# Twenty identity products of TensorE between the two portions of a layer's last down matrices

## The chip, the cores and the metric

The kernel runs on one core of one Trainium2 chip. The metric is the device time of one execution in microseconds (us). The kernel before took 1609.62 us, the median of 3 runs (1609.38 to 1610.01).

## The reference: what is computed

Two layers of a hybrid decoder trunk work on 256 tokens of width 1024, all in 32-bit floats:

```
h = LayerNorm(alpha * x + Mixer(x))
x = LayerNorm(alpha * h + HierMoE(h))
```

The mixer projects x by one wide matrix, feeds retention and a selected sparse attention, gates and sums the two branches and projects the sum. HierMoE sends each token to one of 4 groups and to 2 of the 8 experts in it; each of the 32 experts is `(silu(x @ w_gate) * (x @ w_up)) @ w_down`, with matrices of 1024 by 512, 1024 by 512 and 512 by 1024.

## The kernel before, in words

The mixer part of a layer is bound by TensorE for most of its length; the weights stream through a ring of tiles and are split into a high and a low part by ScalarE and VectorE.

The expert part goes by quads, four experts at a time. Each expert has 32 slots for its tokens, so four experts fill the 128 columns of TensorE's array, and each matmul of a quad has its own 32 columns. Eight quads make a layer. For each quad the 24 MB of its matrices are loaded by SyncE's queue; `quad_half` multiplies the gate and the up matrices, ScalarE and VectorE make the hidden rows, TensorE transposes them (`bank_g`, then `hidT`), and `quad_half` with stage 2 multiplies the down matrices into `bank_y`, two banks of PSUM. `combine` then adds the weighted rows of the quad to the sum `acc`.

The last quad of a layer differs. `load_last_down` loads the second half of its four down matrices in two portions: first chunk 2 of all four experts (four transfers of 512 KB, counted by `last_in[0]`), then chunk 3 of all four (`last_in[1]`). `last_down` (line 1040 on) waits for one portion, multiplies it, waits for the other and multiplies that: for each chunk, 2 banks times 4 experts. Only after the second portion is multiplied does TensorE tell ScalarE that a bank of results is complete (`y_full`, line 1059); ScalarE copies it (line 1334), `sum_up_last` runs `combine` (line 1035) for each half of the columns, and VectorE's closing normalisation begins with statistics of the sum (line 1558). After layer 1 the normalised rows are transposed (line 873) and start layer 2; after layer 2 they are written out and the kernel ends.

TensorE's instructions run in the order in which they are written. `stay_warm(times, bank, of)` at line 615 exists already: it multiplies the identity (a 128 by 128 tile of the constant table) by itself into a bank that nobody reads. It is called with 19 and 3 at the start of layer 2, with 6 and 3 before the first quad, and with 8 on a cleared tile at the very start. The new call uses `bank_g`; its last reader, the copy of the transposed hidden rows, is over by then.

Of the kernel before, what the change touches and what calls it, by code (L numbers as in the profile page):

```python
# [27 lines left out]
FC = FF // P  # L28
# [133 lines left out]
def build(nc, x_in, w_in, w_ret_o, w_dsa_o, w_out, ln1_g, ln1_b, w_gate, w_up, w_down, ln2_g,  # L162
# [6 lines left out]
    with ctx:  # L169
# [133 lines left out]
        def banks(name):  # L303
# [4 lines left out]
        bank_g, bank_u = psum[:, 4, :], psum[:, 5, :]  # L308
# [33 lines left out]
                    for m, half in matrix_half]  # L342
        first_quad = [homes[v] if v in homes else ring_unit[v]
                      for _, v in sorted(FIRST_HOME.items())]
        first_in = [outside_in[v] if v in homes else unit_in[v]
                    for _, v in sorted(FIRST_HOME.items())]
        row_in = [sem(f"row_in{t}") for t in range(TT)]
        ident_in, table_in = sem("ident_in"), sem("table_in_mixer")
# [70 lines left out]
        def _(sp):  # L419
# [49 lines left out]
            for l in range(DEPTH):  # L469
                for name, i in STREAM.items():  # L470
# [3 lines left out]
                    if i < len(IN_TILES):  # L474
                        _, c, w = IN_TILES[i]
                        src = at(win_v, l)[:, :, c:c + w]
                    else:
                        v = {"dsa": dsa_v, "ret": ret_v, "out": out_v}[name[:3]]
                        n, w = int(name[3]), NB
                        k = KC * int(name[4]) if name[:3] == "ret" else 0  # L480
                        src = at(v, l)[:, k:k + KC, n * NB:(n + 1) * NB]
# [82 lines left out]
        def _(pe):  # L564
# [50 lines left out]
            def stay_warm(times, bank=bank_y[0], of=ident):  # L615

                for _ in range(times):
                    nc.tensor.matmul(bank[:, 0:P], of, of, start=True, stop=True)
# [426 lines left out]
            def last_down():  # L1045

                part = range(5 * QUAD, 6 * QUAD)
                for c in (FC - 2, FC - 1):
                    landed = last_in[c - FC // 2]
                    pe.wait_ge(landed, 16 * QUAD).then_inc(landed, -16 * QUAD)  # L1050
                    for n, bank in enumerate(bank_y):
                        for e, u in enumerate(part):
                            w = later_quad[u].rearrange("p (k n) -> p k n", k=FC // 2)
                            s = slice(e * SLOTS, (e + 1) * SLOTS)
                            mm = nc.tensor.matmul(bank[s, :], hidT[:, c, s],  # L1055
                                                  w[:, c - FC // 2, n * NB:(n + 1) * NB],
                                                  start=False, stop=(c == FC - 1))
                        if c == FC - 1:
                            mm.then_inc(y_full[n], 1)

            def experts(first=False, last=False, tiles=later_quad, landed=later_in):

# [43 lines left out]
                if last:  # L1106
                    last_down()
                else:
                    arrived(2, 1, landed)
                    quad_half(bank_y, hidT, FC, 2, 1, tiles)  # L1110
# [1001 lines left out]
```

## Time and profile before

| what | value |
|---|---|
| median of 3 runs | 1609.62 us (1609.38 to 1610.01) |
| the profiled execution, its own time | 1608.99 us |
| its span, first to last instruction | 1607.2 us |
| mean granted TensorE clock | 0.901 |
| TensorE matmuls busy | 1301.8 us, 81% |
| VectorE busy | 622.6 us, 39% |
| ScalarE busy | 387.9 us, 24% |
| DMA | 524.58 MB, mean 326 GB/s |

A busy share is an average over the whole span, and the stages of this kernel have different limits. In the 40 slices of the page, PE is the busy share of TensorE in tenths, PEclk the granted clock in tenths of full speed (1.00 is 2.4 GHz, 0.50 is 1.2 GHz), and DMA the share of the 16 DMA engines. A 32-bit product appears in the trace as two matmul records, each with its weight load, and is told in records below. A timeline row with "x38" stands for 38 records and its length reaches from the start of the first to the end of the last.

### The profile page before, as it was taken

What the parts mean: (1) busy time and instruction counts of PE and PEld (TensorE: products, weight loads), DVE (VectorE), ACT (ScalarE), POOL (GpSimd) and SP (SyncE); (2) the same over time, 40 slices, a digit from 0 to 9 for tenths busy, and PEclk for the clock granted to TensorE, in tenths of its full rate; (3) what the DMA queues carried; (4) which work ended last, traced back from release to release, by engine and by line L of the source; (5) the groups of instructions that cost most, each with busy time, mean ns of one, the idle gap of its engine ahead of it and who ended that gap; (6) DMA issues with size and microseconds to landing.
All of it is one profiled execution on the core that took longest, in us unless ns stands there. A gap on an engine that the chain in (4) does not pass through costs nothing. (4 is left out here: it accounts for less than half of the span.)

```text
span 1607.2 us, 21340 instructions
## 1 busy us (share of the span) xinstructions
PE 1301.8 (81%) x8678; PEld 883.9 (55%) x8678; DVE 622.6 (39%) x1063; ACT 387.9 (24%) x449; POOL 0.2 (0%) x4
## 2 busy tenths in 40 slices
PE   9999999999856656657799999999997556656665
PEld 8998889995312212222398988899953122212211
DVE  6788686654100100100187876765631000000102
ACT  4334634322100000001143357343220000000000
POOL 0000000000000000000000000000000000000000
PEclk9999999999977878877899999999999778788778
DMA  8555445789999999999954454376999999999996
GB/s 303 171 195 184 159 158 215 262 338 420 426 429 427 427 427 428 429 427 429 404 193 164 158 210 177 115 260 217 385 427 428 427 424 428 426 428 429 427 426 254
DMA packets 95686, 524.58 MB, mean 326 GB/s; under 512 B 5360, under 2 KB 9840, under 8 KB 65920
## 3 DMA queue, kind: packets, MB, share of 16 engines
q1 hardware_dynamic: 94864, 523.10, 80.8%
q8 instruction: 50, 0.82, 0.2%
q10 hardware_dynamic: 752, 0.50, 0.1%
q14 instruction: 20, 0.16, 0.0%
HBM read 522.53 MB, written 1.05 MB: 326 GB/s over the span
## 5 line engine op out<-in xcount | busy, mean ns | idle before, releaser
L1022 PE MATMUL psum<-ring,aqT 128*32 128x512 f32 x1536 | 275.3, 698 | 111.7 <-PEq L1010 111.7
L1672 DVE TENSOR_TENSOR w_low<-ring,w_high 128x2048 fp32r<-128x2048 f32 (+2 forms) x108 | 239.8, 2260 | 71.9 <-DVEq L1671 70.6
L1236 ACT ACTIVATE w_high<-ring 128x2048 fp32r<-128x2048 f32 (+2 forms) x108 | 198.6, 1886 | 193.3 <-ACTq L1232 178.8
L1022 PE MATMUL psum<-spare,aqT 128*32 128x512 f32 x256 | 131.9, 704 | 98.9 <-PEq L1077 98.9
L1909 DVE TENSOR_TENSOR qk<-psum,qk 128x512 f32<-128x512 f32 x16 | 11.1, 692 | 482.2 <-DVEq L1908 482.2
L1022 PEld LDWEIGHTS psum<-ring,aqT 128*32 128x32 f32 x1536 | 71.7, 126 | 214.3 <-issue 214.3
L1022 PE MATMUL psum<-rv,tmp 128*32 128x512 f32 x240 | 123.5, 705 | 68.1 <-PEq L1104 68.1
L701 PE MATMUL psum<-x_high,w_high 128*128 128x256 f32 x512 | 146.9, 287 | 0.0
L701 PE MATMUL psum<-x_high,w_low 128*128 128x256 f32 x512 | 143.4, 280 | 0.0
L701 PE MATMUL psum<-x_low,w_high 128*128 128x256 f32 x512 | 143.3, 280 | 0.0
L608 PE MATMUL psum<-w_high,x_high 128*128 128x512 f32 (+2 forms) x352 | 138.7, 394 | 0.0
L608 PE MATMUL psum<-w_high,x_low 128*128 128x512 f32 (+2 forms) x352 | 136.3, 387 | 0.0
L608 PE MATMUL psum<-w_low,x_high 128*128 128x512 f32 (+2 forms) x352 | 135.7, 385 | 0.0
L1022 PEld LDWEIGHTS psum<-spare,aqT 128*32 128x32 f32 x256 | 29.5, 127 | 188.9 <-issue 188.9
L1022 PE MATMUL psum<-rg,tmp 128*32 128x512 f32 x240 | 123.7, 706 | 0.0
L1022 PE MATMUL psum<-x_xT,tmp 128*32 128x512 f32 x240 | 123.7, 706 | 0.0
L1022 PE MATMUL psum<-ring,tmp 128*32 128x512 f32 x208 | 116.4, 723 | 0.0
L1022 PEld LDWEIGHTS psum<-rv,tmp 128*32 128x32 f32 x240 | 27.8, 127 | 146.1 <-issue 146.1
L701 PEld LDWEIGHTS psum<-x_high,w_high 128*128 128x128 f32 x512 | 96.3, 188 | 2.8 <-issue 2.8
L701 PEld LDWEIGHTS psum<-x_high,w_low 128*128 128x128 f32 x512 | 96.9, 189 | 1.4 <-issue 1.4
L701 PEld LDWEIGHTS psum<-x_low,w_high 128*128 128x128 f32 x512 | 96.0, 188 | 0.0
L1922 DVE TENSOR_TENSOR qk<-qk,psum 128x512 f32<-128x512 f32 x16 | 17.2, 1076 | 188.3 <-DVEq L1920 188.3
(260 smaller groups left out, 2294.4 us busy)
## 6 DMA issues: line engine op xcount, KB each, us to landing
ring<-in_w_gate_dram SPq DMA_DIRECT2D x56, 2048.0 KB, 33.1
ring<-in_w_in_dram SPq DMA_DIRECT2D x34, 2048.0 KB, 7.9
ring<-in_w_up_dram SPq DMA_DIRECT2D x28, 2048.0 KB, 22.2
spare<-in_w_up_dram SPq DMA_DIRECT2D x14, 2048.0 KB, 14.3
rv<-in_w_down_dram SPq DMA_DIRECT2D x12, 2048.0 KB, 31.2
rg<-in_w_down_dram SPq DMA_DIRECT2D x12, 2048.0 KB, 35.6
x_xT<-in_w_down_dram SPq DMA_DIRECT2D x12, 2048.0 KB, 40.1
ring<-in_w_down_dram SPq DMA_DIRECT2D x12, 2048.0 KB, 29.1
```

The source lines that it names most:

```text
L608: mm = nc.tensor.matmul(ps[:, t, 0:w], a, b[:, k, :], start=(k == 0 and m == 0), stop=(k == KC - 1 and m == 2))
L701: mm = nc.tensor.matmul(out, a[:, k, c], v, start=(start and k == 0 and m == 0), stop=(stop and k == KC - 1 and m == 2))
L1022: mm = nc.tensor.matmul(bank[s, :], lhs[:, c, s], w[:, k, n * NB:(n + 1) * NB], start=(c == 0), stop=(c == chunks - 1))
L1236: nc.scalar.activation(half_tile(high, i % HIGH, w, b), half_tile(ring, i % RAW, w, b), ACT.Copy).then_inc(high_ready, 1)
L1672: V.tensor_tensor(half_tile(low, i % RAW, w, b), half_tile(ring, i % RAW, w, b), half_tile(high, i % HIGH, w, b).bitcast(f32), ALU.subtrac ...
L1909: loop_step(V.tensor_tensor(msig, bank_g, msig, ALU.mult))
L1922: V.tensor_tensor(hid.rearrange("p (j q) -> p j q", j=FC), msig.rearrange("p (q j) -> p j q", j=FC), bank_u.rearrange("p (q j) -> p j q", ...
```

## The change

In `last_down`, inside the loop over the two chunks, after the matmuls of the first portion and so ahead of the wait for the second, TensorE is given twenty products of the identity with itself. The call is made once in each layer. Nothing is removed.

```diff
@@ last_down @@
                                                   start=False, stop=(c == FC - 1))
                         if c == FC - 1:
                             mm.then_inc(y_full[n], 1)
+                    if c == FC - 2:
+                        stay_warm(20, bank_g)
```

The function that it calls:

```
            def stay_warm(times, bank=bank_y[0], of=ident):

                for _ in range(times):
                    nc.tensor.matmul(bank[:, 0:P], of, of, start=True, stop=True)
```

## Rows read from the trace of the kernel before

**Rows 1.** The page: span, busy time by engine, and the 40 slices.
```profile
span 1607.2 us, 21340 instructions
PE 1301.8 (81%) x8678; PEld 883.9 (55%) x8678; DVE 622.6 (39%) x1063; ACT 387.9 (24%) x449; POOL 0.2 (0%) x4
PEclk9999999999977878877899999999999778788778
DMA  8555445789999999999954454376999999999996
```

**Rows 2.** The chain that ended last: start us, length us, what.
```profile
1590.59 1.92 PE psum L1055 x16
...
1592.54 3.69 PE psum L1035 x8
...
1603.97 0.75 DVE x_xT L1589
```

**Rows 3.** Timeline of TensorE, end of layer 1: start us, length us, operation.
```profile
789.05 0.59 PE L1055 MATMUL psum<-rv,tmp 128*32 128x512 f32 x1
...
793.02 0.68 PE L1055 MATMUL psum<-rv,tmp 128*32 128x512 f32 x1 [3.35 <-PEq L1050]
...
793.49 1.06 PE L1055 MATMUL psum<-rv,tmp 128*32 128x512 f32 x1
...
794.34 1.06 PE L1055 MATMUL psum<-rv,tmp 128*32 128x512 f32 x1
...
796.28 3.94 PE L1035 MATMUL psum<-qk,aqT 128*128 128x512 f32 x8
800.06 4.40 PE L618 MATMUL psum<-tab 128*128 128x128 f32 x38
804.70 0.63 PE L873 MATMUL psum<-tab,x_xT 128*128 128x128 f32 x4 [0.23 <-PEq L568]
```

**Rows 4.** Timeline of TensorE, end of layer 2.
```profile
1586.92 0.59 PE L1055 MATMUL psum<-rv,tmp 128*32 128x512 f32 x1
...
1587.35 0.59 PE L1055 MATMUL psum<-rv,tmp 128*32 128x512 f32 x1
...
1590.59 0.59 PE L1055 MATMUL psum<-rv,tmp 128*32 128x512 f32 x1 [2.62 <-PEq L1050]
...
1592.54 3.67 PE L1035 MATMUL psum<-qk,aqT 128*128 128x512 f32 x8
```

**Rows 5.** Timeline of VectorE: last statistics of layers 1 and 2.
```profile
800.26 0.70 DVE L1558 BATCH_NORM_STATS2 stat<-psum 128x6 f32<-128x512 f32 x1 [0.16 <-PE psum L1035]
...
1596.25 0.70 DVE L1558 BATCH_NORM_STATS2 stat<-psum 128x6 f32<-128x512 f32 x1 [0.16 <-PE psum L1035]
```

**Rows 6.** Windows: stretch, length, busy us by engine, granted clock, DMA share, GB/s.
```profile
789.50:793.00 3.50, 0.17 (x4) 0.01 (x1) 0.00 (x0) 0.00 (x0) 0.00 (x0) 1.00 1.03 391
793.50:796.50 3.00, 3.00 (x17) 0.75 (x10) 0.00 (x0) 0.60 (x1) 0.00 (x0) 0.50 1.05 385
800.00:804.50 4.50, 4.46 (x39) 4.21 (x37) 4.31 (x23) 0.74 (x1) 0.00 (x0) 1.00 1.07 383
808.00:812.00 4.00, 4.00 (x22) 3.13 (x20) 3.54 (x4) 2.89 (x4) 0.00 (x0) 1.00 0.10 29
1587.90:1590.50 2.60, 0.07 (x4) 0.00 (x0) 0.00 (x0) 0.00 (x0) 0.00 (x0) 1.00 0.47 189
1590.60:1592.50 1.90, 1.90 (x16) 0.46 (x16) 0.00 (x0) 0.60 (x1) 0.00 (x0) 1.00 0.00 0
```

**Rows 7.** Every record of line 618: durations ns min/median/max, first and last start.
```profile
L618 PEld LDWEIGHTS psum<-tab x80: 187/192/193, 366.2 to 1166.7; 128*128 128x128 f32 x80
L618 PE MATMUL psum<-tab x80: 272/275/356, 366.3 to 1166.9; 128*128 128x128 f32 x80
L618 PE MATMUL psum<-tmp x16: 294/421/582, 1.5 to 4.9; 128*128 128x128 f32 x16
```

**Rows 8.** Timeline of layer 2's start: a table load, a weight split, normalised rows.
```profile
796.57 1.64 SPq L447 DMA_DIRECT2D tab<-in_tables_dram  x1
...
798.84 1.90 ACT L1216 ACTIVATE w_high<-ring 128x2048 fp32r<-128x2048 f32 x1
...
803.64 0.75 DVE L1589 SCALAR_TENSOR_TENSOR x_xT<-x_xT,rstd,stage 128x512 f32<-128x512 f32 x1
...
806.37 1.17 PE L628 MATMUL psum<-w_high,x_high 128*128 128x512 f32 x4
```

## The prediction

> **What bounds the kernel now.** I read the 40 slices first [rows 1]. In both layers there is a long stretch in which the DMA digits are 9 and the granted clock is 7 or 8 tenths: the expert part, paced by the loading of its weights. Between them lies a stretch with DMA digits of 4 to 7 and a clock of 9: the mixer, where TensorE sets the pace. The change lies at the end of each expert part, so the second view is the chain that ended last [rows 2]. It has nothing to hide behind in layer 2: the second portion's matmuls (1590.59), the combining matmuls (1592.54), VectorE's normalisation and the output follow one another. Whatever delays 1590.59 delays the end by as much.
>
> The third view is TensorE's timeline around the wait for the second portion, once in each layer. In layer 1 the last records of the first portion start at 789.05 and those of the second at 793.02, after 3.35 us idle [rows 3]. In layer 2 it is 1587.35 and 1590.59, after 2.62 us idle [rows 4]. The two gaps differ in what the clock does behind them. Layer 1: granted clock 1.00 up to 793.0 and 0.50 from 793.5 to 796.5, that is 1.2 GHz. Layer 2: 1.00 through the gap and through the second portion, 2.4 GHz [rows 6]. So there is a clock loss to win back in layer 1 and, in this execution, none in layer 2.
>
> **The change: what the products cost.** Twenty calls are added in each layer. Line 618 shows how many records a call makes: 22 calls in layer 2's start and 9 before the first quad of each of two layers are 40 calls and 80 records [rows 7], so a call is 2 records and twenty are 40. The 38 records from 800.06 last 4.40 us at clock 1.00 [rows 3, 6]. One of them lasts 0.275 us [rows 7], so the pitch is (4.40 - 0.275) / 37 = 0.1115 us, and 40 records take 4.46 us of TensorE. At the low clock the 16 records at the kernel's start (1.5 to 4.9) have a pitch of 3.4 / 15 = 0.23 us, which would make 9.1 us; that is the upper bound. The lower bound is nothing, if all fit into the gap. I take 4.46, from a row of the same instruction on the same tile at the same clock.
>
> The Trainium skill ("TensorE: Matmul & The Clock Gate", section "Back-to-back issue gap") gives about 81 ns for each product of 128 columns in a stream of weight loads and matmuls. By it 40 records would be 3.24 us, which fits into layer 1's gap and nearly into layer 2's, and the sum would be an improvement of 1.1 to 1.2 us. The measured pitch of 0.1115 us decides against it here; whole 32-bit calls cost two such records.
>
> **Layer 1.** The first portion's records have a pitch of 0.43 us per group of four (1586.92 to 1587.35 in layer 2, at the same clock [rows 4]). TensorE is thus free for the products at 789.05 + 0.43 = 789.48, and done with them at 789.48 + 4.46 = 793.94. The second portion, which started at 793.02, starts 0.92 us later. Its weights have landed by then, so the wait for them costs nothing any more; what ends last is the stream of products.
> - The second portion runs at the full clock: from its start to the first combining matmul it takes 1592.54 - 1590.59 = 1.95 us as in layer 2 [rows 4], instead of 796.28 - 793.02 = 3.26 us [rows 3]. Gain 1.31.
> - From the first combining matmul to the last statistics: 800.26 - 796.28 = 3.98 in layer 1, 1596.25 - 1592.54 = 3.71 in layer 2 [rows 3 to 5]. Gain 0.27, since layer 1 began this at the low clock.
> - Sum of layer 1: +0.92 - 1.31 - 0.27 = -0.66 us.
>
> **Does the 0.66 reach the end?** Behind layer 1's sum stand the closing normalisation, the 19 warming calls and the first transposes at 804.70. The rows become ready at 803.64 + 0.75 = 804.39 and the calls end at 800.06 + 4.40 = 804.46 [rows 3, 8]; both count from the combining matmuls and move together. The other inputs of layer 2's start are early: the weight split ends at 798.84 + 1.90 = 800.74 and is used at 806.37 [rows 8], and in 808 to 812 the DMA share is 0.10, so all that was asked for has landed [rows 6]. The one load behind a wait on this quad, the table at 796.57, moves with it. The mixer is then paced by TensorE, and its frees start the expert loads. So I let the whole 0.66 through; the bounds are 0 and 0.66.
>
> **Layer 2.** TensorE is free at 1587.35 + 0.43 = 1587.78, the products end at 1592.24, and the second portion starts 1592.24 - 1590.59 = 1.65 us later. The clock was full there already, so nothing comes back. All of it is on the chain of rows 2: +1.65 us.
>
> Queued behind the products on TensorE are only the wait, the second portion, and the combining matmuls. ScalarE's copies and VectorE's statistics wait for those and are counted in the sums. SyncE waits for nothing that moves, except the table load and the final stores. The code grows by 80 matmuls and 80 weight loads of 8678 each [rows 1], 0.9%; I price its fetching at nothing, with 0.3 us either way as an estimate of what the spread of the three runs (0.63 us) could hide.
>
> **Sum.** -0.66 + 1.65 = +0.99 us. The profiled execution took 1608.99 us (span 1607.2, 1.79 around it), so the changed kernel would take 1609.98 in its place. That execution was 0.63 below the median of the runs shown; the same step on the median is 1609.62 + 0.99 = 1610.6 us.
>
> **Rivals.**
> - *The clock doesn't usually fall in layer 1.* The one trace shows it falling there, but the layer 2 gap, 0.73 us shorter, shows none, so it may be a matter of chance from run to run. For it: the profiled execution, with the fall, was not slower than the three runs. Then nothing is won: +0.92 + 1.65 = +2.57, 1612.2 us. Chance 0.20. A mixture of both kinds of run lies between.
> - *The gain of layer 1 is lost on the way*, in some transfer of layer 2 that does not move: +1.65, 1611.3 us. Against it: the DMA share of 0.10 at 808 to 812. Chance 0.08.
> - *The clock often falls in layer 2 too* in the runs without a profile. Then layer 2 costs 1.65 - 1.58 = +0.07, and the sum is -0.59: 1609.0 us. Against it: 1.00 through the gap. Chance 0.12.
> - *The products take half the time*, one record a call at 0.1115: 2.23 us, inside both gaps (3.35 and 2.62). Then layer 1 wins 1.58 and layer 2 loses nothing: 1608.0 us. Against it: 38 records for 19 calls. Chance 0.04; the case of the skill's 81 ns, about 1608.5 us, has 0.02 beside it.
> - *Slower by more than measurement: the products don't hold the clock.* Were the chip to take them for idleness, the clock would fall while they run, and most of the 40 records would go at 0.23 us. It decides from the moment that the clock falls before the products are through. At worst 9.1 us in each layer: layer 1 starts its second portion at 798.6, +5.6; layer 2 at 1596.9, +6.3, and +1.58 for a low clock behind it: +13.5, 1623 us. Against it: clock 1.00 in 800.0 to 804.5 under 38 such records [rows 6]. Chance 0.03.
>
> **How the numbers follow.** The forecast of +0.99 has 0.51. About 0.2% is what a measurement of this kernel can tell from no change, 3.2 us: 1606.4 to 1612.8. Every case but the last lies inside it. Slower gets 0.04 (the last rival, and a little for the first one with some unpriced cost of 0.6 us on top). Faster gets 0.01: even free products with both layers' clock losses won back give 2 x 1.58 = 3.16 us. Same: 0.95. The range takes in the rivals on both sides, 1609.0 to 1612.3, and leaves out the half-price products and the lost clock.
>
> **What would show it.** In the profile after: 40 records of line 618 between the portions in each layer, of 4.4 to 4.5 us; no idle time that ends in line 1050 at the second portion; granted clock 1.00 from 789 to 800; 1.95 us from the second portion's start to line 1035 in both layers; layer 1's last statistics about 0.7 us earlier than 800.26 and layer 2's about 1 us later than 1596.25. The prediction is wrong if the stream of products is much shorter or longer than 4.46 us, if the clock falls under it, or if layer 2's second portion was waiting for a fall that this trace happened not to have.

## The result and the profile after

The changed kernel takes 1614.65 us (median of 11 runs, 1612.63 to 1616.66), the kernel before 1610.01 us in its 11 runs beside them (1608.13 to 1613.48). The ratio is 1.0025, 95% interval 1.0018 to 1.0033: slower by 4.0 us, 2.9 to 5.3. (The two medians lie 4.64 us apart, inside that interval.) The forecast was 1610.6 us, +0.99, range 1609.0 to 1612.3. So the direction of the forecast sum was right and its size was a quarter of what was measured.

The profiled execution took 1614.56 us, span 1612.8. TensorE's timeline at the end of layer 1 (start us, length us, operation), against [rows 3]:

```profile
791.93 0.59 PE L1055 MATMUL psum<-rv,tmp 128*32 128x512 f32 x1
...
792.47 4.73 PE L618 MATMUL psum<-tab 128*128 128x128 f32 x40
797.13 0.62 PE L1055 MATMUL psum<-rv,tmp 128*32 128x512 f32 x1
...
799.10 3.67 PE L1035 MATMUL psum<-qk,aqT 128*128 128x512 f32 x8
802.60 4.40 PE L618 MATMUL psum<-tab 128*128 128x128 f32 x38
807.24 0.63 PE L873 MATMUL psum<-tab,x_xT 128*128 128x128 f32 x4 [0.23 <-PEq L568]
```

The same at the end of layer 2, against [rows 4]:

```profile
1590.94 0.59 PE L1055 MATMUL psum<-rv,tmp 128*32 128x512 f32 x1
...
1591.48 4.73 PE L618 MATMUL psum<-tab 128*128 128x128 f32 x40
1596.15 0.62 PE L1055 MATMUL psum<-rv,tmp 128*32 128x512 f32 x1
...
1598.11 3.67 PE L1035 MATMUL psum<-qk,aqT 128*128 128x512 f32 x8
```

Neither second portion has an idle mark any more. Its start is set by the 40 records ahead of it. From the start of the first portion's last group of four matmuls to the start of the second portion's first group it is 797.13 - 791.93 = 5.20 us in layer 1 and 1596.15 - 1590.94 = 5.21 in layer 2. I call this time the gap; TensorE's idle time in it is some 0.6 us shorter, since the last group still runs. Before, the gap was 3.97 and 3.24 [rows 3, 4], with 3.35 and 2.62 us idle. In the chain that ended last the products now stand between the two portions (start, length, what), against [rows 2]:

```profile
1589.84 1.72 PE psum L1055 x16
1591.55 4.66 PE psum L618 x40
1596.22 1.85 PE psum L1055 x16
1598.11 3.69 PE psum L1035 x8
```

The windows over the products and the second portion (stretch, length, busy us by engine, granted clock, DMA share, GB/s), against [rows 6]: the clock stays at 1.00, 2.4 GHz, in both layers.

```profile
792.50:797.10 4.60, 4.60 (x44) 4.51 (x40) 0.00 (x0) 0.00 (x0) 0.00 (x0) 1.00 1.05 389
797.10:799.10 2.00, 1.96 (x18) 0.45 (x17) 0.00 (x0) 0.60 (x1) 0.00 (x0) 1.00 1.06 384
...
1591.50:1596.10 4.60, 4.60 (x44) 4.52 (x40) 0.00 (x0) 0.00 (x0) 0.00 (x0) 1.00 0.20 81
1596.10:1598.10 2.00, 1.97 (x18) 0.44 (x17) 0.00 (x0) 0.60 (x1) 0.00 (x0) 1.00 0.00 0
```

Between these two single executions the layer ends explain only part of the 5.57 us. Layer 1: 802.60 - 791.93 = 10.67 us from the first portion's last group to the warming calls, against 800.06 - 789.05 = 11.01 before, 0.34 less. Layer 2: +1.97 in the gap. Together +1.63. Of the remaining 3.94 us, 2.88 were there before the first of the new products ran: the last group of layer 1's first portion started at 791.93 and not at 789.05. The other 1.05 lie in layer 2 ahead of its own products: from the warming calls to the first portion's last group it took 1590.94 - 802.60 = 788.34 us against 1587.35 - 800.06 = 787.29. The question was whether such differences belong to the change (code that grew or moved) or to the execution, and whether one trace gives a fair picture of the gap.

### The profile page after: what moved, and what is told of

Read it like the earlier page. It is cut to its first block and busy times, and to the rows that moved or that the text cites. A ratio compares the mean times of both kernels' runs of the same rounds, so it can differ in the third digit from the quotient of the medians.

```text
span 1612.8 us, 21500 instructions
## 1 busy us (share of the span) xinstructions
PE 1313.6 (81%) x8758; PEld 893.5 (55%) x8758; DVE 622.5 (39%) x1063; ACT 388.1 (24%) x449; POOL 0.2 (0%) x4
## 3 DMA queue, kind: packets, MB, share of 16 engines
HBM read 522.53 MB, written 1.05 MB: 325 GB/s over the span
## 5 line engine op out<-in xcount | busy, mean ns | idle before, releaser
L1022 PE MATMUL psum<-ring,aqT 128*32 128x512 f32 x1536 | 283.4, 713 | 114.3 <-PEq L1010 114.3
L1022 PE MATMUL psum<-spare,aqT 128*32 128x512 f32 x256 | 137.3, 727 | 100.1 <-PEq L1079 100.1
```

Of the source, the lines that this page charges most:

```text
L1022: mm = nc.tensor.matmul(bank[s, :], lhs[:, c, s], w[:, k, n * NB:(n + 1) * NB], start=(c == 0), stop=(c == chunks - 1))
```

## Experiments

Four theories stand in the expectations. A: the clock usually does not fall in layer 1. B: about 2.4 us come from somewhere else, by code that grows or moves. C: the trace of before was typical, the clock falls in layer 1 as a rule. D, formed after the first four runs below: the stream of twenty makes every gap 5.2 us, and the change costs what that is above the natural gap, which varies. The code lines below are shown against the changed kernel, those of the hidden products against the kernel before; gains and losses in us are against the kernel before, with 95% intervals.

**The kernel before, unchanged.**

> The kernel before, unchanged, to see how much one execution differs from the next. Every theory expects a ratio of 1.000 to the kernel before. What it tells is the clock in layer 1's gap. Theory A (the clock usually does not fall there, and the one trace was an exception): granted clock 1.00 from the gap to the combining matmuls, which then start about 1.95 us after the second portion. Theory C (it usually falls): 0.50 again, 3.0 to 3.3 us.

Ratio 1.0002 (0.9992 to 1.0012). TensorE's timeline at the ends of its two layers:

```profile
791.72 0.59 PE L1055 MATMUL psum<-rv,tmp 128*32 128x512 f32 x1
...
794.71 0.59 PE L1055 MATMUL psum<-rv,tmp 128*32 128x512 f32 x1 [2.38 <-PEq L1050]
...
796.66 3.67 PE L1035 MATMUL psum<-qk,aqT 128*128 128x512 f32 x8
...
1589.93 0.59 PE L1055 MATMUL psum<-rv,tmp 128*32 128x512 f32 x1
...
1591.96 0.59 PE L1055 MATMUL psum<-rv,tmp 128*32 128x512 f32 x1 [1.42 <-PEq L1050]
```

The gaps are 2.99 and 2.03 us, not 3.97 and 3.24, and the combining matmuls start 1.95 us after the second portion in layer 1: no fall of the clock, as theory A says. The last group of layer 1's first portion started at 791.72 here, with no change in the code. So the 2.88 us by which the changed kernel's trace lagged at that point are within what one execution differs from the next. The 788.34 us in layer 2 are so too: here it is 1589.93 - 800.17 = 789.76.

**Twenty products in one layer only.**

```diff
-                    if c == FC - 2:
+                    if c == FC - 2 and l == 0:        # the other run: l == 1
                         stay_warm(20, bank_g)
```

> The twenty products in layer 1 only. The second portion should start 5.2 us after the last group of the first (4.0 in the kernel before). Theory A (no fall of the clock to win back, as a rule): +1.2 us, ratio 1.0008. Theory C (the clock falls as a rule and the product stream wins it back): -0.3 us, 0.9998. Theory B (about 2.4 us come from somewhere else, by the code that grows or moves, whatever the products do in the gap): +2 us or more, 1.0013 or above.

> The twenty products in layer 2 only. Theories A and C: the second portion starts 5.2 us after the last group of the first instead of 3.2, all on the chain that ends last: +2.0 us, ratio 1.0012. Theory B: +2.0 and up to 2.4 more, 1.0025. A ratio near 1.000 would mean that the gap of layer 2 is usually longer than the one trace showed.

Layer 1 only: 1.0021 (1.0012 to 1.0031), +3.4 us (1.9 to 5.0). Layer 2 only: 1.0014 (1.0005 to 1.0022), +2.3 us (0.8 to 3.5). Theory C, which my forecast followed, wanted -0.3 for layer 1 alone and is ruled out. Both layers pay. The layer with products, first in the one run and then in the other:

```profile
792.08 0.59 PE L1055 MATMUL psum<-rv,tmp 128*32 128x512 f32 x1
...
797.28 0.62 PE L1055 MATMUL psum<-rv,tmp 128*32 128x512 f32 x1
```

```profile
1586.53 0.59 PE L1055 MATMUL psum<-rv,tmp 128*32 128x512 f32 x1
...
1591.73 0.62 PE L1055 MATMUL psum<-rv,tmp 128*32 128x512 f32 x1
```

Its gap is 797.28 - 792.08 = 5.20 and 1591.73 - 1586.53 = 5.20 us; the layer without has 1593.13 - 1590.75 = 2.38 and 793.37 - 790.22 = 3.15. For layer 1 alone theory A, as it was written down, expected +1.2 us, which lies below the interval, while theory B's "+2 us or more" lies in it. The 1.2 was 5.20 less the one gap of 4.0; less a gap of 3.0, as traces without products have in the mean, it would be some 2.2 us, which the interval just holds. So this run alone does not tell a shorter natural gap from theory B.

**Ten and five products.**

```diff
-                        stay_warm(20, bank_g)
+                        stay_warm(10, bank_g)        # the other run: 5
```

> Ten products instead of twenty, in both layers: 20 records of 0.117 us, 2.33 us, which end before the second portion has landed (gaps of 3.35 and 2.62 us). All theories of the direct cost: no start is delayed. Theory A: ratio 1.000. Theory C: the clock stays up in layer 1, -1.0 to -1.6 us, 0.999 to 0.9994. Theory B (code that grows or moves costs by itself): slower in spite of it, +1.0 us or more, about half of 2.4.

> Ten products in both layers once more, since the first measurement (0.9991, 0.9982 to 0.9999) promised a version faster than both. Theory D: the second portion starts 2.95 us after the last group of the first or at the landing, whichever is later: +0 to +0.9 us in each layer, and up to 1.6 us back where the clock would have fallen: 0.9995 to 1.0005. If the gain of 1.4 us is real, 0.999 again.

> Five products in both layers: 10 records; by the traces of ten and twenty the second portion can start 2.95 - 10 x 0.1115 = 1.83 us after the last group of the first at the earliest, below every gap seen (2.0 the shortest). Theory D: never late, so at worst 1.000; where the clock is held up in layer 1, up to 1.3 us less, 0.9992 to 1.000. Theory B: half of a quarter of 2.4 us more, 1.0004.

> Five products in both layers once more. Theory D: never late, and it wins what a falling clock costs, 1.58 us, in as many ends of a layer as it falls in (2 of the 10 seen without products): 0.6 us in the mean, ratio 0.9996. If it beats the kernel before by more than that, 0.999.

Ten: 0.9991 (0.9982 to 0.9999), then 0.9995 (0.9986 to 1.0004). Five: 0.9994 (0.9985 to 1.0003), then 1.0003 (0.9994 to 1.0012). The first result for ten looked like a gain of 1.4 us; repeated, it is not clear of no change, and no version is shown to beat the kernel before. What is clear is that half the products cost nothing measurable where twenty cost 4 us. The first of these runs was expected to end its stream before the second portion lands, and this missed: with ten, the stream is just about as long as the gap. It set both starts itself there, in layer 1 so:

```profile
791.81 0.59 PE L1055 MATMUL psum<-rv,tmp 128*32 128x512 f32 x1
...
794.78 0.62 PE L1055 MATMUL psum<-rv,tmp 128*32 128x512 f32 x1
```

The second run's layer 2 waited 0.20 us more:

```profile
1587.45 0.59 PE L1055 MATMUL psum<-rv,tmp 128*32 128x512 f32 x1
...
1588.00 2.50 PE L618 MATMUL psum<-tab 128*128 128x128 f32 x20
1590.69 0.59 PE L1055 MATMUL psum<-rv,tmp 128*32 128x512 f32 x1 [0.20 <-PEq L1050]
```

The first run's gaps were 794.78 - 791.81 = 2.97 and 1591.00 - 1588.03 = 2.97 us. So ten make 2.97 and twenty 5.20, 0.223 us for each product, and none would make 2.97 - 10 x 0.223 = 0.74. Theory B wanted a loss of 1.0 us or more with ten and about 0.6 with five; the intervals of ten, -2.9 to -0.2 and -2.3 to 0.6 us, exclude it, and those of five, which end at 0.5 and 1.9 us, decide little. In the eight layer ends of these four runs, with gaps of 2.51 to 3.24 us, the granted clock stayed at 1.00.

**The same twenty products where nothing waits for them.**

```diff
                 if last:
                     spread_second()
+                    stay_warm(20, bank_g)
                 arrived(0, 0, landed)
```

> The same twenty products in each layer, written where TensorE waits some 8 us for the gate matrices of the last quad, and not between the portions: the code grows by as much, and nothing waits for them. Theory B (code that grows or moves costs by itself): slower, ratio 1.001 to 1.0015. Theory D (the twenty products make the time from the first portion's last group to the second portion 5.18 us in every execution, and the change costs 5.18 minus the gap that the weights' landing leaves, 2.0 to 4.0 us in the eight layer ends seen without a later start): ratio 1.000 here, and gaps of 2 to 4 us again in both layers.

Ratio 1.0004 (0.9995 to 1.0013), +0.6 us (-0.8 to 2.1). The same number of records is added, ahead of the last quad's gate matrices. Here they run in part at the low clock (granted 0.50 in 1546.1 to 1550.0) and take 7.12 us, the first half of the gate matmuls follows, and then TensorE still waits 7.20 us for the second half, where the kernel before waited 8.17:

```profile
1546.07 7.12 PE L618 MATMUL psum<-tab 128*128 128x128 f32 x40 [1.29 <-PEq L1004]
...
1567.39 1.03 PE L1022 MATMUL psum<-spare,aqT 128*32 128x512 f32 x1 [7.20 <-PEq L1078]
```

It rules out theory B at its full 2.4 us. The 1.0010 at the lower end of what B expected still lies in the interval, so a smaller cost of the code, under 2.1 us, is not excluded by this run. The gaps are 793.81 - 791.22 = 2.59 and 1589.83 - 1586.96 = 2.87.

**The kernel before, a third and a fourth time.**

> The kernel before, unchanged, for a further look at its gaps and its clock. Theory D: the gap from the last group of the first portion to the second portion is 2.0 to 4.0 us in both layers, about 3.0 in the mean in layer 1 and 2.6 in layer 2. Theory C (the gap of layer 1 is usually 4 us and the clock falls): 3.9 us, 0.50.

> The kernel before, unchanged, for another two gaps. Theory D: 2.0 to 4.0 us, about 3.1 in layer 1 and 2.8 in layer 2; a low clock only behind a long one, over 3.3 us, for which the two seen were 3.95 and 3.46.

Ratios 0.9998 (0.9988 to 1.0008) and 1.0002 (0.9993 to 1.0011). Both had a short gap in layer 1 (792.64 - 789.90 = 2.74 and 794.18 - 791.24 = 2.94) and a long one in layer 2, and in both the clock fell behind the long one. The first:

```profile
1586.21 0.59 PE L1055 MATMUL psum<-rv,tmp 128*32 128x512 f32 x1
...
1589.69 0.59 PE L1055 MATMUL psum<-rv,tmp 128*32 128x512 f32 x1 [2.86 <-PEq L1050]
...
1591.20 1.06 PE L1055 MATMUL psum<-rv,tmp 128*32 128x512 f32 x1
...
1592.28 4.61 PE L1035 MATMUL psum<-qk,aqT 128*128 128x512 f32 x8
```

Its windows, and VectorE's last statistics:

```profile
1589.70:1590.70 1.00, 1.00 (x12) 0.45 (x16) 0.00 (x0) 0.00 (x0) 0.00 (x0) 1.00 0.06 16
1590.70:1593.60 2.90, 2.90 (x14) 0.80 (x3) 0.00 (x0) 1.19 (x2) 0.00 (x0) 0.51 0.01 3
```

```profile
1596.93 0.70 DVE L1558 BATCH_NORM_STATS2 stat<-psum 128x6 f32<-128x512 f32 x1 [0.16 <-PE psum L1035]
```

From the second portion to the last statistics it is 1596.93 - 1589.69 = 7.24 us here, 800.26 - 793.02 = 7.24 in layer 1 of the first trace of before, and 1596.25 - 1590.59 = 5.66 where the clock stayed [rows 3 to 5]. A fall costs 1.58 us whichever layer it comes in. The fourth trace has a gap of 1590.94 - 1587.50 = 3.44 in layer 2, the same fall, and the same 1598.18 - 1590.94 = 7.24 to its last statistics:

```profile
1591.90:1594.80 2.90, 2.90 (x14) 0.87 (x7) 0.00 (x0) 1.19 (x2) 0.00 (x0) 0.53 0.01 3
```

**Forty products in layer 2.**

```diff
-                    if c == FC - 2:
-                        stay_warm(20, bank_g)
+                    if c == FC - 2 and l == 1:
+                        stay_warm(40, bank_g)
```

> Forty products, in layer 2 only. Theory D: the second portion starts 0.72 + 40 x 0.223 = 9.64 us after the last group of the first (2.95 with ten, 5.18 with twenty), against gaps of 2.0 to 3.5 us without products in that layer, mean 2.8: +6.9 us, less about 0.3 for a clock that sometimes falls there: ratio 1.0041. Theory B: no more per product than 2.4/40 us beside it, which can't be told from D here.

Ratio 1.0051 (1.0037 to 1.0066), +8.2 us (6.0 to 10.6); expected +6.6, inside. The gap is as computed:

```profile
1587.99 0.59 PE L1055 MATMUL psum<-rv,tmp 128*32 128x512 f32 x1
...
1588.54 9.20 PE L618 MATMUL psum<-tab 128*128 128x128 f32 x80
1597.66 0.62 PE L1055 MATMUL psum<-rv,tmp 128*32 128x512 f32 x1
```

1597.66 - 1587.99 = 9.67, against 0.74 + 40 x 0.223 = 9.66. Twice the products cost more of the kernel's time, all in one place on the chain. The remaining gap, in layer 1, was 794.85 - 792.18 = 2.67.

## Why the prediction was wrong

Thirteen layer ends without products between the portions are now seen. Layer 1: 3.97, 2.99, 2.74, 2.94, 2.59, 3.15, 2.67, mean 3.01. Layer 2: 3.24, 2.03, 3.48, 3.44, 2.87, 2.38, mean 2.91. The clock fell behind 3.97, 3.48 and 3.44 and behind no gap of 3.24 or less. The sum by these:

| term | forecast | by the runs |
|---|---|---|
| gap with the products, each layer | 0.43 + 4.46 = 4.89 | 5.20 |
| natural gap, layer 1 | 3.97 | 3.01 |
| natural gap, layer 2 | 3.24 | 2.91 |
| clock won back, both layers | 1.58 | 2 x 3/13 x 1.58 = 0.73 |
| change of the time | +0.99 | 2.19 + 2.29 - 0.73 = +3.75 |

+3.75 stands against a measured 4.0 (2.9 to 5.3). The forecast was 2.76 us below this sum: 1.29 by the two gaps, 0.85 by the clock, 0.62 by the seams. The thirteen gaps scatter by about 0.5 us each and three falls are few, so the sum itself is good to about half a microsecond, an estimate from that scatter.

The same means give +1.8 us for products in layer 1 alone, +1.9 for layer 2 alone and +6.4 for forty in layer 2. Measured were +3.4 (1.9 to 5.0), +2.3 (0.8 to 3.5) and +8.2 (6.0 to 10.6): all three above the sum, the first just beyond its interval. A further cost of about a microsecond is therefore not excluded. No experiment isolates it; the hidden products (+0.6, -0.8 to 2.1) and the ten (no loss in either run) leave little room for a cost of the code alone.

- *The products' stream.* The count of 40 records and their pitch of 0.1115 us were right, and the clock stayed at 1.00 under them. What I left out are the seams, 0.31 us in each layer, 0.6 in all. I let the first product follow the last group of four after 0.43 us, as one group follows another, and the second portion follow the last product just as closely. The first product follows after 792.47 - 791.93 = 0.54. Its weight load starts only then, while between groups the loads run ahead:

```profile
791.52 0.11 PEld L1055 LDWEIGHTS psum<-ring,tmp 128*32 128x32 f32 x1
792.47 4.54 PEld L618 LDWEIGHTS psum<-tab 128*128 128x128 f32 x40 [0.84 <-issue]
797.13 0.11 PEld L1055 LDWEIGHTS psum<-rv,tmp 128*32 128x32 f32 x1
```

  From the first product to the second portion it is then 797.13 - 792.47 = 4.66 instead of 4.46; the load of the second portion also starts only with its matmul.
- *The delay of the second portion* ("+0.92" in layer 1, "+1.65" in layer 2) is the step that failed most. It subtracted the gap of one execution, and that execution had the longest gap of layer 1 that any trace shows, 0.96 above the mean, and one 0.33 above the mean in layer 2. In the mean the delays, seams included, are 2.19 and 2.29 us. The mechanism was right: the traces show that the start is set by whichever comes last, the end of the stream or the landing.
- *The clock won back* ("Gain 1.31", "Gain 0.27") had the right size where a fall comes, 1.58 us, but I charged it to every execution. It came in 1 of 7 ends of layer 1, and in 2 of 6 of layer 2, where I had written that nothing comes back. The long gap and the fall belong together, so the one trace was wrong on both terms in the same direction.
- *Passing through to the end.* The path I argued for holds: from the combining matmuls to the first transposes and on to the first 448-wide projection the intervals of all traces agree within 0.05 us, apart from the fall itself; from there to layer 2's first expert matmul, 350.2 to 350.5 us later, within 0.3 us. From that matmul to the last group of layer 2's first portion it is 418.3 to 419.4 us in twelve traces and 420.9 in the first repeat, so a delay of layer 1 isn't made up in the expert part either. Products in layer 1 alone cost 3.4 us (1.9 to 5.0) at the end.
- *Code size at nothing.* Not contradicted: +0.6 (-0.8 to 2.1) for the hidden products, no loss with ten.
- *The rivals.* The first, that the clock usually does not fall in layer 1, was the true case for the clock; its +2.57 was too low since it kept the two long gaps and left out the seams. The second, a gain lost on the way, is excluded by the intervals just given. The third, a fall in layer 2, came in 2 of 6 ends, but in no trace together with a fall in layer 1, as its 1609.0 us needed. Half-price products and products under a low clock are excluded by the rows of line 618. The Trainium skill's 81 ns a product ("TensorE: Matmul & The Clock Gate", section "Back-to-back issue gap"), cited in the forecast, is not what this trace shows for these records: 0.1115 us each, with weight loads of 0.19 us in the stream.
- *The chances.* "Same" had 0.95 and slower 0.04. The point 1.0025 is beyond the 0.2% stated there, and its interval, 1.0018 to 1.0033, begins just below that. With the gap taken as 2.0 to 4.0 us, slower by over 0.2% would have been the likelier side.

Why the gap varies from 2.0 to 4.0 us is only partly shown. The first portion's matmuls and the second portion's landing move apart: in the four traces of the kernel before, the last group of layer 1's first portion started at 789.05, 791.72, 789.90 and 791.24, and the second portion at 793.02, 794.71, 792.64 and 794.18. The former spread over 2.7 us and the latter over 2.1. What shifts the transfers against each other was not tested.

One more thing stays open. In the six traces with products between the portions of layer 1 that last group started at 791.12 to 792.29, in the seven without at 789.05 to 792.18, in the mean 1.0 us earlier. It lies ahead of the first new product, and thirteen executions don't tell whether it is chance.

## What to carry to other kernels

A gap that ends with a transfer is not one number: read it in several executions before subtracting it, above all when a clock fall sits behind it, because the long gap and the fall come together and the pair is the exception. Filler work in front of a wait should be sized to the shortest gap, seams included, or it becomes the wait; here ten calls (2.97 us) were free within measurement and twenty (5.20 us) cost 4 us. The most that the filler can win, if it holds the clock at all, is the cost of the fall times how often it comes, here 1.58 us in 3 of 13.

## What the hardware showed that was not expected

- A full-width product behind matmuls that each use 32 columns starts 0.54 us after the last group's start instead of 0.43, its weight load no longer runs ahead, and the way back adds 0.20 us: 0.31 us for the pair of seams. Whether the width, the tile or the bank of PSUM makes the seam was not tested.
- The clock of TensorE fell 0.4 to 1.1 us after work had resumed behind gaps of 3.44, 3.48 and 3.97 us (2.84, 2.86 and 3.35 us idle), and not behind 3.24 us (2.62 idle): in the third trace 1.00 from 1589.7 to 1590.7 and 0.51 from 1590.7 to 1593.6, quoted above. What it costs falls on the work that follows the gap.
- Five calls were already followed by gaps of 2.51 to 2.99 us without a fall, but so were gaps of that length without any products. Whether five calls would hold the clock in a long gap is open.
